# Where column-form weight blocks stand in their buffer slots: one place for all, or seven places in turn

## The chip, the cores and the metric

The kernel runs on one core of one Trainium2 chip. The metric is device time in microseconds from one launch to its end; the kernel before was run three times and took 2912.8, 2912.95 and 2913.8 us, median 2912.95. The profile is of one execution of the same program.

## The reference

The program computes two transformer-like layers on 256 tokens of width 2048, in float32. What matters here is that nearly all of the arithmetic is a token matrix times a weight matrix:

```python
h = rms_norm(x, norm_g);  proj = h @ w_in                # 2048 x 16512, split into 15 parts
ya = chunked_band_attention(aq, ak, av, a_rel_bias) * silu(az)
yb = rwkv7_time_mix(br, bk, bv, ...) * silu(bz)          # heads of 64, a scan over the tokens
yc = memory_cross_attention(cq, mk, mv) * silu(cz)       # mk, mv = rms_norm(mem) @ w_mem_kv
merged = sigmoid(ga)*(ya @ w_up_a) + sigmoid(gb)*(yb @ w_up_b) + sigmoid(gc)*(yc @ w_up_c)
x = x + merged @ w_o
# second layer: h @ w_in_2, block attention, gated linear attention, short convolution,
# three up-projections, w_out_2, then
x = x + (silu(h2 @ w_ffn_gate_2) * (h2 @ w_ffn_up_2)) @ w_ffn_down_2
return rms_norm_2(x, final_norm_w_2)
```

## The kernel before, in words

All weights are streamed once through four buffer slots. `plan_stream` (from line 57) writes the list of 128 blocks, each the product of all 256 tokens with up to 512 columns of one weight matrix; a block is cut into units, 976 in all, and unit n uses slot n modulo 4. For each unit SyncE loads float32 weights into `w_raw` (line 463), ScalarE rounds them into `w_hi` (`hi`, line 653), VectorE subtracts to get the remainder `w_lo` (`lo`, line 1058), and TensorE multiplies. Each product is three matmuls in the fp32r format: high weights by high activations, high by low, and low by high. ScalarE is told to prepare unit n + 3 while TensorE works on unit n, so the weights are ready ahead.

Blocks come in two forms. In 98 blocks of the kind `rows` the activations are the stationary operand and 512 weight columns move through the array (lines 1668 to 1670). In the other 30 blocks, the column form (kinds `wide`, `pair`, `trio` and `narrow`), a 128 x 128 tile of weights is loaded as the stationary operand and the 256 tokens move (lines 1677 to 1679). The column form gives 1,696 triples, 5,088 matmuls and as many weight loads.

A slot of `w_hi` or `w_lo` is 1,088 float32 elements (4,352 bytes) per partition, 64 more than a unit fills. `in_slot` (line 235) says where in the slot a unit's weights begin: `SHIFT` puts the `rows` kind at element 0 and the four column kinds at element 16, which is 64 bytes. ScalarE's output, both VectorE's operand and output, and TensorE's reads go through `in_slot`. The tensors begin at multiples of 512 (`w_hi`) and 256 bytes (`w_lo`), each weight tile is 512 bytes wide, so every column-form tile begins at a multiple of 64 bytes. `w_raw` is always filled and read from its slot's beginning.

The order of TensorE's work is written out by hand: between the steps of the recurrent part and of the attentions, `fill` issues units of the stream, or quarters of units (`planned_quarters`, line 1683). Waits on semaphores stand at the head of units and before the small matmuls of those parts. Nothing in the order depends on `in_slot`.

Of the kernel before, what the change touches and what calls it, by code (L numbers as in the profile page):

```python
# [48 lines left out]

SHIFT = {'rows': 0, 'wide': 16, 'pair': 16, 'trio': 16, 'narrow': 16}

DMAS = {"wide": 1, "rows": 1, "pair": 2, "trio": 2, "narrow": 1}

# [111 lines left out]
def build(nc, dram, out):  # L167
    blocks, phases, units, first = plan_stream()
# [5 lines left out]
    def last_unit(m):  # L174
        return first[m + 1] - 1 if m + 1 < len(first) else n_units - 1

    with ExitStack() as ctx:
        sem_of = {}

# [51 lines left out]
        def unit_size(n):  # L231
            k, tiles = KINDS[blocks[units[n][0]].kind]
            return k * tiles * P

        def in_slot(w, n):
            at = SHIFT[blocks[units[n][0]].kind]
            return w[:, n % RING, at:at + unit_size(n)]

        def tiles4_of(v, j):
# [11 lines left out]
        v1, v2, at = {}, {}, 0  # L251
        for name, rows in ROWS1:
            v1[name], at = at, at + rows
        n_rows1, at = at, 0
# [384 lines left out]
        def _(act):  # L639
# [7 lines left out]
            def hi(n):  # L647
                slot = n % RING
                if n >= RING:
                    act.wait_ge(sem("unit_used"), n - RING + 1)  # L650
                act.wait_ge(sem(f"landed{slot}"), landed[n])
                size = unit_size(n)
                act.activation(in_slot(w_hi, n), w_raw[:, slot, 0:size], ACT.Copy).then_inc(sem("hi_done"), 1)  # L653
# [385 lines left out]
        def _(dve):  # L1039
# [14 lines left out]
            def lo(n):  # L1054
                slot = n % RING
                dve.wait_ge(sem("hi_done"), n + 1)
                size = unit_size(n)
                dve.tensor_tensor(in_slot(w_lo, n), w_raw[:, slot, 0:size], in_slot(w_hi, n).bitcast(F32), ALU.subtract)\  # L1058
                    .then_inc(sem("lo_done"), 1)
# [575 lines left out]
        def _(pe):  # L1635
# [6 lines left out]
            def unit(n, part=None):  # L1642
# [18 lines left out]
                for j in sorted({j for j, _ in steps}):  # L1661
                    k = u * k_tiles + j
                    if b.kind == "rows":
                        wh, wl = (in_slot(w, n)[:, j * 512:(j + 1) * 512] for w in (w_hi, w_lo))
                        for a in [a for i, a in steps if i == j]:
                            o = gp[:, s, a * 512:(a + 1) * 512]
                            xh, xl = (x[k][:, a * P:(a + 1) * P] for x in (x_hi, x_lo))
                            pe.matmul(o, xh, wh, start=(k == 0), stop=False)  # L1668
                            pe.matmul(o, xl, wh, start=False, stop=False)  # L1669
                            ins = pe.matmul(o, xh, wl, start=False, stop=(k == last_k))  # L1670
                        continue
                    for c in [c for i, c in steps if i == j]:
                        o = gp[:, s, c * T:(c + 1) * T]
                        at = (j * tiles + c) * P
                        wh, wl = (in_slot(w, n)[:, at:at + P] for w in (w_hi, w_lo))

                        pe.matmul(o, wh, x_hi[k], start=(k == 0 and c % 2 == 0), stop=False, skip_group_check=True)  # L1677
                        pe.matmul(o, wh, x_lo[k], start=False, stop=False, skip_group_check=True)  # L1678
                        ins = pe.matmul(o, wl, x_hi[k], start=False, stop=(k == last_k), skip_group_check=True)  # L1679
# [422 lines left out]
```

## Time and profile before

| | before |
|---|---|
| runs | 2912.8, 2912.95, 2913.8 us; median 2912.95 |
| the profiled execution, first to last instruction | 2913.4 us |
| TensorE busy | 2882.6 us, 99% |
| VectorE, ScalarE busy | 1619.3 us (56%), 1344.1 us (46%) |
| mean granted TensorE clock | 0.999 |
| DMA | 518.30 MB, mean 178 GB/s |

The span of the profiled execution lies inside the range of the three runs, and no other time of it is recorded, so a change worked out against the span is taken off the median as it stands. TensorE's matmuls are pipelined and overlap in the profile: the duration of one (0.28 us for 256 columns) holds its whole way through the array, while the distance between the starts of two neighbours is what one costs. The two have to be kept apart below.

### The profile page before, as it was taken

What the parts mean: (1) busy time and instruction counts of PE and PEld (TensorE: products, weight loads), DVE (VectorE), ACT (ScalarE), POOL (GpSimd) and SP (SyncE); (2) the same over time, 40 slices, a digit from 0 to 9 for tenths busy, and PEclk for the clock granted to TensorE, in tenths of its full rate; (3) what the DMA queues carried; (4) which work ended last, traced back from release to release, by engine and by line L of the source; (5) the groups of instructions that cost most, each with busy time, mean ns of one, the idle gap of its engine ahead of it and who ended that gap; (6) DMA issues with size and microseconds to landing.
All of it is one profiled execution on the core that took longest, in us unless ns stands there. A gap on an engine that the chain in (4) does not pass through costs nothing.

```text
span 2913.4 us, 42709 instructions
## 1 busy us (share of the span) xinstructions
PE 2882.6 (99%) x18228; PEld 2491.1 (86%) x18228; DVE 1619.3 (56%) x1860; ACT 1344.1 (46%) x1533; POOL 73.7 (3%) x173
## 2 busy tenths in 40 slices
PE   7999999999999999999999999999999999999998
PEld 7979888888988888889998899888888888888886
DVE  5565665656656556564555466554654544544444
ACT  5452543544554454454455454444444444444443
POOL 5000000001000000000000000000000000000000
PEclk9999999999999999999999999999999999999999
DMA  7443444566665655566556566666566666666564
GB/s 211 125 143 112 134 128 118 166 195 184 227 194 184 189 163 185 191 188 182 174 161 202 166 174 174 196 194 195 192 184 195 188 193 188 188 189 206 192 194 152
DMA packets 356178, 518.30 MB, mean 178 GB/s; under 512 B 18288, under 2 KB 137220, under 8 KB 355220
## 3 DMA queue, kind: packets, MB, share of 16 engines
q1 hardware_dynamic: 355220, 512.37, 58.7%
q0 software_dynamic: 768, 3.20, 0.4%
q8 instruction: 143, 2.34, 0.3%
q14 instruction: 47, 0.39, 0.0%
HBM read 513.39 MB, written 2.11 MB: 177 GB/s over the span
## 4 chain that ended last, share of the span: by engine, by line
PE 98%; DVE 1%; ACT 0%; DMA 0%; issue 0%; SPq 0%; DVEq 0%; ACTq 0%
PE gp L1668 23%; PE gp L1670 23%; PE gp L1669 23%; PE gp L1677 7%; PE gp L1679 7%; PE gp L1678 7%; PE ps L1845 4%; PE ps L1727 1%; PE ps L1802 1%; PE ps L1833 1%; DMA gain<-in_norm_g 0%; PE ps L1787 0%; PE ps L1823 0%; PE ps L2045 0%; PE ps L2062 0%; PE ps L2053 0%
## 5 line engine op out<-in xcount | busy, mean ns | idle before, releaser
L1058 DVE TENSOR_TENSOR w_lo<-w_raw,w_hi 128x1024 fp32r<-128x1024 f32 (+2 forms) x976 | 1166.2, 1202 | 949.6 <-ACT w_hi L653 944.7
L653 ACT ACTIVATE w_hi<-w_raw 128x1024 fp32r<-128x1024 f32 (+2 forms) x976 | 1011.0, 1041 | 1106.4 <-PE gp L1670 877.7
L1668 PE MATMUL gp<-w_hi,h_hi 128*128 128x512 f32 x2112 | 833.5, 395 | 1.5 <-DVE w_lo L1058 1.5
L1670 PE MATMUL gp<-w_lo,h_hi 128*128 128x512 f32 x2112 | 822.7, 390 | 0.0
L1669 PE MATMUL gp<-w_hi,h_lo 128*128 128x512 f32 x2112 | 822.2, 389 | 0.0
L1677 PE MATMUL gp<-h_hi,w_hi 128*128 128x256 f32 x1696 | 488.4, 288 | 1.8 <-DVE h_lo L1123 1.8
L1678 PE MATMUL gp<-h_lo,w_hi 128*128 128x256 f32 x1696 | 474.5, 280 | 0.0
L1679 PE MATMUL gp<-h_hi,w_lo 128*128 128x256 f32 x1696 | 474.3, 280 | 0.0
L1668 PEld LDWEIGHTS gp<-w_hi,h_hi 128*128 128x128 f32 x2112 | 396.6, 188 | 83.8 <-DVE w_lo L1058 1.9
L1670 PEld LDWEIGHTS gp<-w_lo,h_hi 128*128 128x128 f32 x2112 | 396.5, 188 | 83.3
L1669 PEld LDWEIGHTS gp<-w_hi,h_lo 128*128 128x128 f32 x2112 | 396.8, 188 | 80.5 <-issue 0.5
L1677 PEld LDWEIGHTS gp<-h_hi,w_hi 128*128 128x128 f32 x1696 | 321.0, 189 | 8.9 <-issue 4.5
L1678 PEld LDWEIGHTS gp<-h_lo,w_hi 128*128 128x128 f32 x1696 | 321.8, 190 | 1.1 <-issue 0.5
L1679 PEld LDWEIGHTS gp<-h_hi,w_lo 128*128 128x128 f32 x1696 | 319.9, 189 | 0.0
L1668 PE MATMUL gp<-w_hi,y_hi 128*128 128x512 f32 x448 | 175.3, 391 | 0.0
L1670 PE MATMUL gp<-w_lo,y_hi 128*128 128x512 f32 x448 | 174.4, 389 | 0.0
L1669 PE MATMUL gp<-w_hi,y_lo 128*128 128x512 f32 x384 | 149.4, 389 | 0.0
L1668 PE MATMUL gp<-w_hi,f_hi 128*128 128x512 f32 x352 | 137.0, 389 | 0.0
L1670 PE MATMUL gp<-w_lo,f_hi 128*128 128x512 f32 x352 | 136.9, 389 | 0.0
L1669 PE MATMUL gp<-w_hi,f_lo 128*128 128x512 f32 x352 | 136.9, 389 | 0.0
L1845 PEld LDWEIGHTS ps<-arena 64*64 64x64 f32 x3072 | 102.8, 134 | 19.0 <-issue 10.5
L1845 PE MATMUL ps<-arena 64*64 64x32 f32 (+2 forms) x3072 | 114.7, 225 | 0.0
(290 smaller groups left out, 1805.3 us busy)
## 6 DMA issues: line engine op xcount, KB each, us to landing
w_raw<-in_w_in SPq DMA_DIRECT2D x384, 512.0 KB, 4.0
w_raw<-in_w_ffn_gate SPq DMA_DIRECT2D x88, 512.0 KB, 4.4
w_raw<-in_w_ffn_up SPq DMA_DIRECT2D x88, 512.0 KB, 4.4
w_raw<-in_w_ffn_down SPq DMA_DIRECT2D x88, 512.0 KB, 4.1
w_raw<-in_w_in SPq DMA_DIRECT2D x136, 256.0 KB, 3.2
w_raw<-in_w_in SPq DMA_DIRECT2D x128, 192.0 KB, 3.1
w_raw<-in_w_mem_kv SPq DMA_DIRECT2D x32, 512.0 KB, 4.3
w_raw<-in_w_o SPq DMA_DIRECT2D x32, 512.0 KB, 4.3
```

Source lines behind the costliest of these rows:

```text
L653: act.activation(in_slot(w_hi, n), w_raw[:, slot, 0:size], ACT.Copy).then_inc(sem("hi_done"), 1)
L1058: dve.tensor_tensor(in_slot(w_lo, n), w_raw[:, slot, 0:size], in_slot(w_hi, n).bitcast(F32), ALU.subtract)\
L1668: pe.matmul(o, xh, wh, start=(k == 0), stop=False)
L1669: pe.matmul(o, xl, wh, start=False, stop=False)
L1670: ins = pe.matmul(o, xh, wl, start=False, stop=(k == last_k))
L1677: pe.matmul(o, wh, x_hi[k], start=(k == 0 and c % 2 == 0), stop=False, skip_group_check=True)
L1678: pe.matmul(o, wh, x_lo[k], start=False, stop=False, skip_group_check=True)
L1679: ins = pe.matmul(o, wl, x_hi[k], start=False, stop=(k == last_k), skip_group_check=True)
L1727: ins = pe.transpose(cross[e % 2][:, c * T + a * P:c * T + (a + 1) * P], src[:, a, c * P:(c + 1) * P], ident[:])
L1802: ins = pe.matmul(ps[:, 2 + g % 2, tt * T + keys.start:tt * T + keys.stop], q[:, h * dt + d, tt * P:(tt + 1) * P], k[:, h * dt + d, 0:keys ...
L1833: ins = pe.matmul(psB[:, d * T + t0:(d + 1) * T], v[:, kt, at:at + P], pt[:, kt * T:(kt + 1) * T - t0], start=(kt == 0), stop=(kt == 1), s ...
L1845: ins = pe.matmul(out[hh], left[hh], right[hh], start=(i == 0), stop=(i == len(terms) - 1))
```

## The change

The table by kind is replaced by a list of places that the column-form blocks take in turn, in the order of the stream. The `rows` kind stays at element 0.

```diff
-SHIFT = {'rows': 0, 'wide': 16, 'pair': 16, 'trio': 16, 'narrow': 16}
+COLUMN_PLACES = (16, 15, 17, 14, 18, 13, 19)
...
+    place, columns = [], 0
+    for b in blocks:
+        place.append(0 if b.kind == "rows" else COLUMN_PLACES[columns % len(COLUMN_PLACES)])
+        columns += b.kind != "rows"
...
         def in_slot(w, n):
-            at = SHIFT[blocks[units[n][0]].kind]
+            at = place[units[n][0]]
             return w[:, n % RING, at:at + unit_size(n)]
```

In bytes the places are 64, 60, 68, 56, 72, 52 and 76. Of the 5,088 column-form matmuls 624 keep element 16; 864 go to element 15 and 720 each to 17, 14, 18, 13 and 19. Within a block the place is one and the same. The instructions of every engine, their order, sizes and waits stay as they are; only start addresses in `w_hi` and `w_lo` differ. The four `q_cols` blocks of the second layer, which follow each other without anything between them, are at 19, 16, 15 and 17.

## Rows read from the trace of the kernel before

**Rows 1.** The page: busy us, share of the span, instructions.
```profile
PE 2882.6 (99%) x18228; PEld 2491.1 (86%) x18228; DVE 1619.3 (56%) x1860; ACT 1344.1 (46%) x1533; POOL 73.7 (3%) x173
```
**Rows 2.** Waits of TensorE, whole span: total us, times, longest.
```profile
PE ps L1727 <- DVE arena L1136: 14.4, 2, 13.8
PE gp L1677 <- DVE h_lo L1123: 1.8, 2, 1.1
PE gp L1668 <- DVE w_lo L1058: 1.5, 1, 1.5
```
**Rows 3.** Groups by line: busy us, mean ns | idle before.
```profile
L1677 PE MATMUL gp<-h_hi,w_hi 128*128 128x256 f32 x1696 | 488.4, 288 | 1.8 <-DVE h_lo L1123 1.8
L1678 PE MATMUL gp<-h_lo,w_hi 128*128 128x256 f32 x1696 | 474.5, 280 | 0.0
L1679 PE MATMUL gp<-h_hi,w_lo 128*128 128x256 f32 x1696 | 474.3, 280 | 0.0
```
**Rows 4.** Timeline, start us and us, block of stream at 34 us.
```profile
34.37 0.28 PE L1677 MATMUL gp<-h_hi,w_hi 128*128 128x256 f32 x1
34.48 0.28 PE L1678 MATMUL gp<-h_lo,w_hi 128*128 128x256 f32 x1
...
50.69 0.28 PE L1677 MATMUL gp<-h_hi,w_hi 128*128 128x256 f32 x1
```
**Rows 5.** Timeline, the four `q_cols` blocks, entry from row form and last matmul.
```profile
1288.38 0.39 PE L1670 MATMUL gp<-w_lo,h_hi 128*128 128x512 f32 x1
1288.60 0.28 PE L1677 MATMUL gp<-h_hi,w_hi 128*128 128x256 f32 x1
...
1378.94 0.28 PE L1679 MATMUL gp<-h_hi,w_lo 128*128 128x256 f32 x1
```
**Rows 6.** Line 1678 alone, by stretches: from:to, length, PE busy (count), weight loads.
```profile
31.00:54.00 23.00, 17.92 (x65) 12.07 (x65) 1.00 0.83 229
54.00:101.00 47.00, 33.72 (x120) 22.80 (x120) 1.00 0.59 173
240.00:311.00 71.00, 35.95 (x128) 24.05 (x128) 1.00 0.42 123
1288.00:1379.00 91.00, 71.83 (x256) 49.15 (x256) 1.00 0.65 189
1664.00:1820.00 156.00, 106.92 (x384) 72.79 (x384) 1.00 0.60 166
```
**Rows 7.** Groups in 1288 to 1379 us.
```profile
L1678 PEld LDWEIGHTS gp<-h_lo,w_hi 128*128 128x128 f32 x256 | 49.1, 192 | 0.0
L1677 PEld LDWEIGHTS gp<-h_hi,w_hi 128*128 128x128 f32 x256 | 48.1, 188 | 0.0
L1679 PEld LDWEIGHTS gp<-h_hi,w_lo 128*128 128x128 f32 x256 | 48.1, 188 | 0.0
L1058 DVE TENSOR_TENSOR w_lo<-w_raw,w_hi 128x1024 fp32r<-128x1024 f32 x33 | 40.4, 1225 | 50.5 <-ACT w_hi L653 50.5
L653 ACT ACTIVATE w_hi<-w_raw 128x1024 fp32r<-128x1024 f32 x32 | 33.9, 1058 | 44.8 <-PE gp L1679 44.8
```
**Rows 8.** Timeline, entry from row form at 337 us.
```profile
337.04 0.39 PE L1670 MATMUL gp<-w_lo,h_hi 128*128 128x512 f32 x1
337.27 0.28 PE L1677 MATMUL gp<-h_hi,w_hi 128*128 128x256 f32 x1
```
**Rows 9.** Timeline, row form at 2690 us.
```profile
2690.37 0.39 PE L1670 MATMUL gp<-w_lo,f_hi 128*128 128x512 f32 x1
...
2691.73 0.39 PE L1670 MATMUL gp<-w_lo,f_hi 128*128 128x512 f32 x1
```
**Rows 10.** Groups whose operand starts off a 16-byte boundary, each above one aligned.
```profile
L674 ACT ACTIVATE xr<-gp 128x768 f32<-128x768 f32 x8 | 6.5, 810 | 13.8 <-PE gp L1679 13.8
L706 ACT ACTIVATE arena<-gp 128x768 f32<-128x768 f32 x8 | 6.5, 812 | 6.1 <-PE gp L1679 6.1
L1854 PE MATMUL ps<-xr,gain 128*128 128x256 f32 x16 | 4.7, 378 | 0.0
L2068 PE MATMUL ps<-arena,ones 128*128 128x256 f32 x16 | 4.1, 378 | 0.0
L1297 DVE TENSOR_TENSOR arena<-arena 128x260 f32<-128x260 f32 x8 | 3.4, 429 | 0.3
L1101 DVE TENSOR_TENSOR arena<-arena 128x256 f32<-128x256 f32 x8 | 3.4, 424 | 4.6 <-ACT arena L706 4.6
```
**Rows 11.** Busy of all engines in the densest column stretch, as rows 6 with DVE, ACT, POOL.
```profile
54.00:101.00 47.00, 47.00 (x429) 46.60 (x429) 35.02 (x58) 35.21 (x46) 0.00 (x0) 1.00 0.59 173
```

## The prediction, before the changed kernel was run

> **What bounds the kernel now.** I read the page's busy line first: TensorE is busy 99% of the span, VectorE 56%, ScalarE 46% [rows 1]. The waits of TensorE say the same from the other side: beyond the 14.4 us at the start there are 1.8 and 1.5 us of waiting, so almost nothing is late [rows 2]. The end is therefore set by the pace at which TensorE starts matmuls. The groups by line show three column-form lines of 1,696 matmuls each, 280 to 288 ns long [rows 3], but those durations overlap; the cost is the distance between starts, and for that I went to the timeline.
>
> There the column form turns out to have two paces. From 34.37 to 50.69 us stand 144 matmuls: 16.32 us / 144 = 113.3 ns each [rows 4]. From 1288.60 to 1378.94 us stand the 768 matmuls of the four `q_cols` blocks, 767 distances in 90.34 us: 117.8 ns each [rows 5]. The difference is 4.45 ns. Both stretches are at the full clock (1.00 in rows 6, which is 2.4 GHz), so it isn't the clock. The modelled duration of line 1678 tells the paces apart too: 17.92 / 65 = 276 ns in the quick stretch, 71.83 / 256 = 281 ns in the slow one [rows 6]. From 54 to 101 us it is 33.72 / 120 = 281, from 240 to 311 us 35.95 / 128 = 281, and from 1664 to 1820 us 106.92 / 384 = 278, a mixture [rows 6]. The slow pace also shows in the weight loads: in the slow `q_cols` stretch the load of line 1678 takes 192 ns and those of 1677 and 1679 take 188 [rows 7]. One load in three is held up by some 4 ns.
>
> A pace, once taken, stays: nothing changes it over 767 distances and four blocks. It is taken anew where TensorE restarts behind small matmuls or comes over from the row form, and both outcomes occur: from the row form at 1288.60 it becomes the slow one [rows 5], at 337.27 the quick one [rows 8]. Over the whole trace I counted 4,965 distances between neighbouring column-form matmuls: 1,934 of 113 to 115 ns, 2,840 of 116 to 119 ns and 191 others (restarts); their first and last kinds are those of rows 4 and 5. So the slow pace costs today 2,840 x 4.45 ns = 12.6 us, and the quick one would turn into a loss of 1,934 x 4.45 = 8.6 us if it were lost. The row form has one pace: from 2690.37 to 2691.73 us six matmuls, 227 ns each [rows 9]. It is not touched.
>
> **The change, part by part.** No instruction is added, removed or moved, on any engine or queue, and no wait. `w_raw` and its DMAs keep their addresses. What changes is where 4,464 of the 5,088 column-form weight tiles start (5,088 less the 624 that stay at element 16): by 4 to 12 bytes off a multiple of 64, and for all of them off a multiple of 16.
>
> ScalarE's write of `w_hi` and VectorE's read and write. In the `q_cols` stretch they take 1,058 and 1,225 ns per unit and stand idle 44.8 and 50.5 us of 91 [rows 7]; a unit of 24 matmuls takes TensorE 24 x 117.8 = 2.83 us. Unaligned ones are in the trace: ScalarE's evacuation at line 674 writes rows that begin one element past a boundary and takes 810 ns against 812 ns for the same shape at line 706; VectorE's 128 x 260 at line 1297, whose rows are 65 elements apart, takes 429 ns, and 128 x 256 at line 1101 424 ns, which is the difference of four elements [rows 10]. I take 0. Even 10% more (0.11 and 0.12 us per unit) is hidden under the rest of the 2.83 us. In the densest column stretch VectorE and ScalarE have 12 of 47 us free [rows 11], and its 16 units of 1.22 us there would ask for 2 us more. If that cover were gone, TensorE's wait for `w_lo` is what would grow; it is 1.5 us in all now [rows 2].
>
> TensorE's moving operand. The tokens keep their address. An unaligned moving operand is in the trace, `lora_x` at line 1854, 8 bytes past a 16-byte boundary: 378 ns, as line 2068 with an aligned one [rows 10]. This says that such a start need cost nothing, but of the other operand.
>
> TensorE's weight loads, the one open price. Every stationary operand of before starts on a 16-byte boundary, so no row shows the changed one. From below: the load is not what TensorE waits for, since loads of 188 ns are started every 113 ns and the next is fetched under the matmul; the price of being unaligned is then 0, and if the place breaks up the slow pace it is a gain of at most 12.6 us. From above: the only row in which something about a load costs time is the held-up one, and what hangs on it is 4.45 ns a matmul; one such step more for every moved tile is 4,464 x 4.45 = 19.9 us. I take 0, the value of the nearest row in kind (line 1854, the same engine reading the same memory unaligned), and keep -12.6 and +19.9 as ends.
>
> A rule of the Trainium skill speaks against the change. The rows say that the unaligned operands of the trace cost nothing [rows 10]. The page "SBUF — State Buffer", under "Specifications (TRN2)", says that the memory is read in lines of 16 bytes and that each crossing into a new line is paid for. A tile of 128 floats that begins on a line touches 32 lines, one that begins beside it touches 33, so by that rule each moved load would get longer by about a thirty-second. The trace doesn't agree for the moving operand and is silent on the stationary one.
>
> The paces themselves. The step from one block to the next now shifts the weights by 1 to 6 elements against the tokens, so the one thing that kept the pace over a block's end, that nothing changes, is gone there. I expect the pace to be taken anew at such steps and otherwise as now. Outside `q_cols` the present record is 1,934 quick to 2,840 - 767 = 2,073 slow, 48% quick. Redrawing these blocks with the same odds changes nothing on average. The `q_cols` blocks, one bad draw for four blocks now, become four draws: 767 x 0.48 x 4.45 ns = 1.6 us gained. By chance the sum over some 28 full blocks of about 170 counted distances varies by the root of 28 x half of 170 x 4.45 ns = 2.0 us.
>
> Sum: 0 (ScalarE, VectorE) + 0 (loads) - 1.6 (paces) = -1.6 us, 2913.4 to 2911.8 us of span; the span lies 0.45 us above the median of the runs, so the forecast is 2912.95 - 1.6 = **2911.3 us**, own range 2908 to 2915.
>
> **The rivals.** (A) *An unaligned weight load collides and the slow pace wins*; this ends slower. Its place is the weight load under a running matmul in 25 of 30 blocks. For it: one load in three already is held up in the slow pace [rows 7], and the quick pace needs a fit between two streams that the aligned start may give. Against it: line 1854, and 188 ns loads leave no sign of being near a limit. It decides once more than some 5.8 us are lost, which is 1,300 of the 1,934 quick distances. If only the quick pace is lost: +8.6 us, 2921.6 us. With one more step for every moved tile: +19.9 us, 2932.9 us. In the middle, 2927 us. By the page's line rule it would be this rival that comes true; it has the chance of this rival, since the rule gives no other time.
>
> (B) *The moved start frees TensorE from the slow pace*, at block steps or throughout; this ends clearly faster. For it: the quick pace is the one that the streams can have, the slow one has a period of three matmuls that a small shift could break, and two of the longest slow stretches (54 to 101 and 1288 to 1379 us) run over block ends that are now steps. Against it: inside a block nothing steps, and the slow pace was taken within a few matmuls of the entry at 1288.60 [rows 5]. At most 12.6 us, 2900.3 us; it has to free 1,300 of 2,840 slow distances to leave the band of no change. Middle: 2903.8 us.
>
> (C) *The place has no part in it.* The pace is taken by when TensorE restarts, not by addresses, and the same paces return: 2913 us. For it: in every column block the place was the same 64 bytes, and both paces occurred. Against it: nothing in the trace, which has never had another place.
>
> **How the numbers follow.** Forecast 34%, C 10%, A 28%, B 28%. A measurement of this kernel tells 0.2%, or 5.8 us, from no change. The forecast with its own range and C fall within it: same 0.44; A is slower, 0.28; B is faster, 0.28. For the range I go down to all of B (2900) and up into A to 2928, a little over its middle; what is left out is the upper part of A, some 12%, and a few in a hundred of surprises below.
>
> **What would show it.** Right: distances of 113 and 118 ns and nothing else in the column form, the counts moved by a few hundred, with a change of pace now found exactly at block ends inside 1288 to 1379 us; line 1678 near 280 ns; ScalarE's and VectorE's means at 1,058 and 1,225 ns within 1%; row form at 227 ns. Rival A: loads above 188 ns in blocks off element 16, distances of 118 ns or a third value there, and the 624 at element 16 as before. Rival B: `q_cols` at 113 ns and line 1678 near 276 ns overall. Rival C: all paces, stretch by stretch, as before. I am wrong altogether if the difference lies in the row form or in waits of TensorE.

## The result, and the profile after

The changed kernel takes 2919.42 us (median of 16 runs, 2918.23 to 2920.65) against 2914.16 us for the kernel before (16 runs, 2912.80 to 2915.27): 5.3 us more. The ratio is 1.0019 with a 95% interval of 1.0012 to 1.0026. It is slower, by just less than the 0.2% that the prediction called no change, and not 1.6 us faster. In its runs the time is 1.7 us above the span of the core (2918.68 us against 2917.0 for the profiled one).

The page of the changed kernel, busy us and share of the span per engine, to be read against [rows 1]:

```profile
span 2917.0 us, 42709 instructions
...
PE 2884.4 (99%) x18228; PEld 2492.8 (85%) x18228; DVE 1619.6 (56%) x1860; ACT 1344.6 (46%) x1533; POOL 71.9 (2%) x173
```

TensorE still fills the span. Its waits, against [rows 2] (total us, times, longest):

```profile
PE ps L1732 <- DVE arena L1141: 15.8, 2, 14.3
PE gp L1682 <- DVE h_lo L1128: 2.1, 3, 1.2
PE gp L1673 <- DVE w_lo L1063: 1.5, 1, 1.5
```

Lines are numbered five higher than before. The wait for `w_lo` is the same 1.5 us, so the two engines that write the weights are not late. Their groups, with those of the column form (busy us, mean ns | idle before; ScalarE's and VectorE's first):

```profile
L1063 DVE TENSOR_TENSOR w_lo<-w_raw,w_hi 128x1024 fp32r<-128x1024 f32 (+2 forms) x976 | 1166.4, 1202 | 952.9 <-ACT w_hi L658 948.4
L658 ACT ACTIVATE w_hi<-w_raw 128x1024 fp32r<-128x1024 f32 (+2 forms) x976 | 1011.4, 1041 | 1109.1 <-PE gp L1675 879.3
...
L1682 PE MATMUL gp<-h_hi,w_hi 128*128 128x256 f32 x1696 | 488.7, 288 | 2.1 <-DVE h_lo L1128 2.1
L1683 PE MATMUL gp<-h_lo,w_hi 128*128 128x256 f32 x1696 | 474.6, 280 | 0.0
L1684 PE MATMUL gp<-h_hi,w_lo 128*128 128x256 f32 x1696 | 474.5, 280 | 0.0
```

ScalarE and VectorE write and read the moved weights in the same 1,041 and 1,202 ns as before (their lines in the page of before have the same means). The matmuls' durations over the whole run, 288 and 280 ns, are also those of [rows 3]: a mean over 1,696 of them does not show the loss. The distances between starts do, and the four `q_cols` blocks, one pace of 117.8 ns before [rows 5], show how. The timeline of the changed kernel, start us and duration, at the first matmul of the first, third and fourth of these blocks and at the last of all:

```profile
1289.33 0.28 PE L1682 MATMUL gp<-h_hi,w_hi 128*128 128x256 f32 x1
...
1332.87 0.29 PE L1682 MATMUL gp<-h_hi,w_hi 128*128 128x256 f32 x1
...
1355.82 0.28 PE L1682 MATMUL gp<-h_hi,w_hi 128*128 128x256 f32 x1
...
1378.42 0.28 PE L1684 MATMUL gp<-h_hi,w_lo 128*128 128x256 f32 x1
```

At elements 19 and 16, 384 distances take 43.54 us, 113.4 ns each. At element 15, 192 take 22.95 us, 119.5 ns. At element 17, 191 take 22.60 us, 118.3 ns. The pace changes exactly at the ends of blocks, and 119.5 and 118.3 are paces that the kernel before doesn't have. Taken block by block the durations follow: 276 ns at elements 19 and 16 (from 1290 to 1332 us) and 282 ns at element 15 (from 1332.9 to 1355.7 us). The weight loads don't stand out, 189 ns each in the block at 15. The groups of these two stretches, mean ns behind the busy time:

```profile
L1683 PE MATMUL gp<-h_lo,w_hi 128*128 128x256 f32 x125 | 34.5, 276 | 0.0
...
L1683 PE MATMUL gp<-h_lo,w_hi 128*128 128x256 f32 x65 | 18.3, 282 | 0.0
...
L1682 PEld LDWEIGHTS gp<-h_hi,w_hi 128*128 128x128 f32 x64 | 12.1, 189 | 0.0
L1683 PEld LDWEIGHTS gp<-h_lo,w_hi 128*128 128x128 f32 x64 | 12.1, 189 | 0.0
```

Over the whole stream, distances from 105 to 135 ns, averaged per place, against those of the same blocks before:

| element | distances | same blocks before, ns | after, ns | product, us |
|---|---|---|---|---|
| 13 | 677 | 116.3 | 114.7 | -1.1 |
| 14 | 684 | 116.0 | 117.9 | +1.3 |
| 15 | 825 | 116.0 | 119.5 | +2.9 |
| 16 | 589 | 116.9 | 115.5 | -0.9 |
| 17 | 692 | 116.4 | 118.4 | +1.4 |
| 18 | 683 | 114.9 | 118.3 | +2.3 |
| 19 | 694 | 116.0 | 114.8 | -0.8 |

The sum is +5.1 us, against 5.3 us between the medians. Places 14, 15, 17 and 18 lose 7.9 us and places 13, 16 and 19 give back 2.8. The row form keeps its pace: its 8,824 distances from one row-form matmul to the next add up to 0.01 us more than before.

The two profiled spans differ by only 3.6 us. About 1 us more went into the start and the waits of the changed kernel (its wait for `arena` is 15.8 us against 14.4), and 2.5 us went the other way in the first 10 us of matmuls. Two units of the first block ran at double distance in the profiled execution of before. Its timeline:

```profile
18.57 0.41 PE L1678 MATMUL gp<-h_lo,w_hi 128*128 128x256 f32 x1
18.78 0.41 PE L1679 MATMUL gp<-h_hi,w_lo 128*128 128x256 f32 x1
18.99 0.41 PE L1677 MATMUL gp<-h_hi,w_hi 128*128 128x256 f32 x1
```

and that of the changed kernel:

```profile
19.02 0.28 PE L1683 MATMUL gp<-h_lo,w_hi 128*128 128x256 f32 x1
19.14 0.28 PE L1684 MATMUL gp<-h_hi,w_lo 128*128 128x256 f32 x1
19.26 0.28 PE L1682 MATMUL gp<-h_hi,w_hi 128*128 128x256 f32 x1
```

Twenty such distances were 213 ns before and 113 to 122 after. Of the kernels below, the profiles of those with element 19 or 17 everywhere have all twenty, those with 13 or 15 have none, and those with 22 everywhere or with 16, 13 and 19 in turn have ten, so I count it as no part of the change. It may be why the runs of one kernel lie in groups some 1 us apart: the profiled run of 19 everywhere, with twenty, is the slowest of its nine, but one profile per kernel doesn't prove it.

### The profile page after: what moved, and what is told of

Read it like the earlier page. It is cut to its first block, busy times and chain, and to the rows that moved or that the text cites. A ratio compares the mean times of both kernels' runs of the same rounds, so it can differ in the third digit from the quotient of the medians.

```text
span 2917.0 us, 42709 instructions
## 1 busy us (share of the span) xinstructions
PE 2884.4 (99%) x18228; PEld 2492.8 (85%) x18228; DVE 1619.6 (56%) x1860; ACT 1344.6 (46%) x1533; POOL 71.9 (2%) x173
## 4 chain that ended last, share of the span: by engine, by line
PE 98%; DVE 1%; ACT 0%; DMA 0%; issue 0%; SPq 0%; DVEq 0%; ACTq 0%
PE gp L1673 23%; PE gp L1675 23%; PE gp L1674 23%; PE gp L1682 7%; PE gp L1684 7%; PE gp L1683 7%; PE ps L1850 4%; PE ps L1732 1%; PE ps L1807 1%; PE ps L1838 1%; DMA gain<-in_norm_g 0%; DVE w_lo L1063 0%; PE ps L1792 0%; PE ps L1828 0%; PE ps L2050 0%; PE ps L2067 0%
## 5 line engine op out<-in xcount | busy, mean ns | idle before, releaser
L1063 DVE TENSOR_TENSOR w_lo<-w_raw,w_hi 128x1024 fp32r<-128x1024 f32 (+2 forms) x976 | 1166.4, 1202 | 952.9 <-ACT w_hi L658 948.4
L658 ACT ACTIVATE w_hi<-w_raw 128x1024 fp32r<-128x1024 f32 (+2 forms) x976 | 1011.4, 1041 | 1109.1 <-PE gp L1675 879.3
L1850 PE MATMUL ps<-arena 64*64 64x32 f32 (+2 forms) x3072 | 114.7, 225 | 0.0
```

The costliest lines, as they stand in the source:

```text
L1850: ins = pe.matmul(out[hh], left[hh], right[hh], start=(i == 0), stop=(i == len(terms) - 1))
```

## The experiments

The theory to test was that each place has paces of its own (P). The rivals were that it is changing places that costs (S), and that any start off a 16-byte line costs (L). All kernels below are the changed one with the edit shown.

**One place for all column-form blocks.**

```diff
-COLUMN_PLACES = (16, 15, 17, 14, 18, 13, 19)
+COLUMN_PLACES = (13,)      # and (19,), (15,), (17,)
```

Element 13: 

> Every column-form block at element 13. Theory P (each place has its own pace, whatever stood before it): the pace that the blocks at 13 have in the changed kernel, 114.7 ns a matmul against 116.0 in the kernel before, over 4,840 distances: 6.5 us less than before, about 2907.5 us, and no third pattern. Rival S (the steps from place to place cost, a constant place costs nothing): like the kernel before, 2914 us within 2. Rival L (a start off a 16-byte line costs): slower than before, the same for 13, 15, 17 and 19, by 3.6 to 20 us.

Element 19: 

> Every column-form block at element 19. Theory P: 114.8 ns a matmul as the blocks at 19 in the changed kernel, 6 us less than before, about 2908 us. Rival S: 2914 us within 2. Rival L: slower than before by the same as with 13, 15 and 17.

Element 15: 

> Every column-form block at element 15. Theory P: 119.5 ns a matmul everywhere, so 3.4 ns x 4,840 = 16.5 us more than before, about 2930.5 us. Rival S: 2914 us within 2. Rival L: slower, but by no more than with 13 and 19.

Element 17: 

> Every column-form block at element 17. Theory P: 118.4 ns a matmul everywhere, 11 us more than before, about 2925 us. Rival S: 2914 us within 2. Rival L: the same as 13, 15 and 19.

Measured, with the runs of the kernel before on the same chip at 2913.75 us: 13 took 2913.30 us (ratio 0.9998, 0.9989 to 1.0007), 19 took 2906.09 us (0.9974, 0.9964 to 0.9983), 15 took 2929.32 us (1.0052, 1.0036 to 1.0069), and 17, one run, 2926.64 us. The mean distances over all blocks were 116.05, 114.29, 119.45 and 118.36 ns. The `q_cols` blocks of each, first and last of 768 matmuls; element 13:

```profile
1284.41 0.28 PE L1682 MATMUL gp<-h_hi,w_hi 128*128 128x256 f32 x1
...
1376.44 0.28 PE L1684 MATMUL gp<-h_hi,w_lo 128*128 128x256 f32 x1
```

Element 19:

```profile
1286.64 0.28 PE L1682 MATMUL gp<-h_hi,w_hi 128*128 128x256 f32 x1
...
1373.58 0.28 PE L1684 MATMUL gp<-h_hi,w_lo 128*128 128x256 f32 x1
```

Element 15:

```profile
1293.44 0.28 PE L1682 MATMUL gp<-h_hi,w_hi 128*128 128x256 f32 x1
...
1385.09 0.28 PE L1684 MATMUL gp<-h_hi,w_lo 128*128 128x256 f32 x1
```

Element 17:

```profile
1292.98 0.28 PE L1682 MATMUL gp<-h_hi,w_hi 128*128 128x256 f32 x1
...
1383.74 0.28 PE L1684 MATMUL gp<-h_hi,w_lo 128*128 128x256 f32 x1
```

That is 120.0, 113.4, 119.5 and 118.3 ns. Theory P holds and both rivals fall: the four differ by 23 us with no change of place in any of them, so S is out, and 13 and 19 are off a 16-byte line like 15 and 17, yet reach 113.3 ns. The profile also corrects a detail of the theory. Element 15 and element 17 have one pace each: the blocks' means are 119.3 to 119.6 and 118.3 to 118.5 ns. Elements 13, 16 and 19 have two: 113.3 or 120.0 at 13 and 19, 113.3 or 117.8 at 16, taken within some twelve matmuls of the entry into a stretch and then kept (in the traces of the kernel before and of 13 and 19 everywhere, none of the 42 stretches of 36 and more distances changes its pace after that). That is why 13 missed its expected 2907.5 us by 6 us: the `q_cols` blocks alone, 767 distances at 120.0 and not 113.3, are 5.1 us. One more rival can be read from these traces: that the writes of ScalarE and VectorE into the shifted slots disturb TensorE. In the `q_cols` blocks of the kernel before, the changed one and these four, the mean distance while ScalarE or VectorE is busy is within 0.3 ns of the mean while it is idle, so the differences of 5 to 7 ns are not theirs.

**Are the steps harmless?**

```diff
-COLUMN_PLACES = (16, 15, 17, 14, 18, 13, 19)
+COLUMN_PLACES = (16, 13, 19)
```

> The change with its four slow places taken out: column-form blocks in turn at 16, 13 and 19. If the loss of the change is in the places 14, 15, 17 and 18 and not in changing places: 115.0 ns on average (115.5, 114.7 and 114.8 in the changed kernel), 5 us less than before, about 2909 us. If it is in changing places: as the changed kernel, 2919 us.

Measured 2907.84 us (before 2913.62; ratio 0.9981, 0.9971 to 0.9990), 114.9 ns on average. The step from place to place costs nothing that can be seen; taking out the four slow places (14 and 18 among them, which were not run alone) takes out the loss, with a gain on top.

**Is it the distance between weights and tokens, or the weights' own address?**

```diff
-COLUMN_PLACES = (16, 15, 17, 14, 18, 13, 19)
+COLUMN_PLACES = (17,)
...
-        h_hi = sb("h_hi", [P, KD, T], F32R, align=ROW // 2)
+        h_hi = sb("h_hi", [P, KD * T + 1], F32R, align=ROW // 2)[:, 1:].rearrange("p (a b) -> p a b", b=T)
```

and the same for `h_lo`. (Two small tensors were moved between them. By the tensors' sizes `h_lo` begins 64 elements later for it, 65 with the shift, so for its product the distance to the weights is kept only up to 64 elements; for the two products with `h_hi` it is kept exactly.)

> Column-form weights at element 17 and the tokens (h_hi, h_lo) one element past a 256-byte boundary, so that the weights stand 16 elements ahead of the tokens as in the kernel before, while their own address is that of the run with 17 everywhere. Theory R (the distance between weights and tokens decides): the column form shows the paces of place 16, 113.3 and 117.8 ns, nothing at 118.3 alone. Rival A (the weights' own address decides): 118.3 ns as with 17 everywhere, about 2926 us. The row form reads the shifted tokens as its weights; it stays at 226.7 ns if only the column form is sensitive.

Measured, one run: 2971.97 us beside 2914.76 for the kernel before, far above either expectation. The column form took 120.9 ns on average, 121.1 in the `q_cols` blocks: neither the 113.3 and 117.8 of theory R nor the 118.3 of rival A. Both fall as put. Of the 57.2 us of loss, 33.2 are in the row form's 8,824 distances, where the shifted tokens are the loaded operand. The timeline of this kernel, a row-form block that reads them, and one that reads `f_hi` and `f_lo`, which had not been moved:

```profile
2696.28 0.39 PE L1673 MATMUL gp<-w_hi,h_hi 128*128 128x512 f32 x1
...
2717.89 0.40 PE L1673 MATMUL gp<-w_hi,h_hi 128*128 128x512 f32 x1
...
2779.35 0.39 PE L1673 MATMUL gp<-w_hi,f_hi 128*128 128x512 f32 x1
...
2838.51 0.39 PE L1673 MATMUL gp<-w_hi,f_hi 128*128 128x512 f32 x1
```

The first is 93 distances in 21.61 us, 232.4 ns; the second 261 in 59.16 us, 226.7 ns, the pace of [rows 9]. Within one kernel and one form of matmul, the products with a shifted operand are the ones that are some 6 ns slower. Over 6,158 distances the mean with `h` is 232.4 ns. So the addresses of both operands of a matmul matter, and neither alone nor their distance alone gives the pace.

**The row form's place.**

```diff
-        place.append(0 if b.kind == "rows" else ...)
+        place.append((0, 3, 13, 16, 19, 32, 1)[(len(place) - columns) % 7] if b.kind == "rows" else ...)
```

with the column form at 19.

> Row-form blocks in turn at elements 0, 3, 13, 16, 19, 32 and 1, column form at 19. If the row form's 226.7 ns is a floor and its loads never meet the moving stream badly, every place runs at 226.7 ns and the time is that of 19 everywhere, 2906 us. If the row form has bad places too, some blocks run slower by about 4 to 6 ns a matmul, up to 3 us for a block of 96 matmuls in 100 us of stream, and the whole is later by 10 to 40 us.

Measured, one run: 2943.72 us, 37.6 us above 19 everywhere, so the second of the two. Means per place: 0: 227.3 ns; 19: 228.3; 3: 229.0; 16: 230.8; 32: 232.7; 13: 233.4; 1: 236.6. A block at element 1, the timeline of this kernel:

```profile
2868.13 0.40 PE L1673 MATMUL gp<-w_hi,f_hi 128*128 128x512 f32 x1
...
2929.89 0.40 PE L1673 MATMUL gp<-w_hi,f_hi 128*128 128x512 f32 x1
```

261 distances in 61.76 us, 236.6 ns against 226.7. Here the shifted operand is the one that moves, and it costs 10 ns. Element 0, where the kernel has its rows, is the best of the seven.

**Other places for the column form.** Three runs with seven places each, `COLUMN_PLACES = (0, 8, 12, 20, 22, 24, 32)` and the like.

> Column-form blocks in turn at elements 0, 8, 12, 20, 22, 24 and 32. It is read for the pace of each place. If the order seen so far (13, 16 and 19 can run at 113.3 ns, 14, 15, 17 and 18 never do) goes on in threes, 22 can run at 113.3 ns and 20 and 24 cannot. If what matters is nearness to 16, all seven run at one pace. If a start off a 16-byte line costs, only 22 is slower.

> Column-form blocks in turn at elements 10, 11, 21, 23, 28, 40 and 48, for the pace of each. In threes: 10, 28 and 40 can run at 113.3 ns, and 11, 21, 23 and 48 cannot. By nearness to 16: all alike. By 16-byte lines: 28, 40 and 48 quicker than the others.

> Column-form blocks in turn at elements 5, 25, 29, 35, 45, 51 and 54, for the pace of each. If the paces repeat every 32 elements (48 had those of 16, and 32 that of 0), 45, 51 and 54 have those of 13, 19 and 22: 113.3 as one pace. If they repeat every 16, 29 and 35 have them too. 5 and 25 have no counterpart that can run at 113.3 ns.

They took 2924.12, 2925.57 and 2925.54 us, one run each. The table has the mean of each place and the share of its distances that stand in a settled quick pace, counted as twelve or more distances of 113 or 114 ns in a row:

| places | share in the settled quick pace | mean, ns |
|---|---|---|
| 22 | 50% | 114.9 |
| 45, 48 | 51%, 37% | 115.8, 116.1 |
| 51 | 22% | 118.7 |
| 35, 11, 24, 8, 23 | none | 117.7, 117.8, 118.0, 118.3, 118.4 |
| 20, 29, 10, 32, 12 | none | 118.7, 118.7, 119.1, 119.2, 119.5 |
| 5, 0, 40, 54, 28, 25, 21 | none | 119.7, 119.8, 119.8, 119.8, 119.9, 119.9, 120.0 |

A mean over four or five blocks is rough: that of 12 is made of blocks near 118 ns and one at 123.2.

The order in threes holds near 16 (22 yes, 20 and 24 no) and fails farther off (10, 28 and 40 no, 48 yes). A repeat every 32 elements fits 48 with 16 and 45 with 13, but 51 only now and then behaves like 19, and 54 is at 120.0 where 22 is at 113.3. A repeat every 16 fits neither 29 nor 35. Rule L fails again: 0, 20, 28, 32 and 40 are on a 16-byte line and slow, 22 and 45 are off it and quick. I have no formula for the pace; that stays open.

**Element 22 everywhere.**

> Every column-form block at element 22. Its blocks in the sweep took 114.9 ns a matmul on average, with 113.3 as one pace and 116 to 118 as the other. If a place keeps its paces and the share of the quick one stays: 1.2 ns x 4,840 = 5.7 us less than before, about 2908 us. If the share is drawn anew, anything from 113.3 (2901 us) to 117.5 ns (2921 us).

Measured 2907.67 us (before 2913.62; ratio 0.9978, 0.9969 to 0.9987), 114.9 ns: as expected with the share kept.

**A version that beats both.**

```diff
-COLUMN_PLACES = (16, 15, 17, 14, 18, 13, 19)
+COLUMN_PLACES = (19, 22, 19, 19, 19, 19, 19, 19, 19, 19, 19, 19, 22, 19, 19, 19, 19, 19, 19, 22, 22, 19, 19, 19, 19, 19, 19, 19, 19, 19)
```

> Element 19 everywhere but in four blocks that ran slowly there (the second of the stream, 120.0 ns; the second of the C columns with silu, 115.1; the last two of the L columns, 115.9 and 116.0), which go to element 22, where they took 113.5, 114.7, 115.0 and 113.7 ns. If a block keeps its pace at its place: 190 distances times 6.5, 0.4, 0.9 and 2.3 ns, 1.9 us less than 19 everywhere, about 2904 us. If the pace is drawn anew at each entry: within 3 us of 2906.

Measured 2904.93 us (5 runs, 2903.32 to 2905.54) beside 2913.65 for the kernel before: ratio 0.9965, 0.9952 to 0.9979, 8.7 us less than before and 14.5 less than the changed kernel. The four blocks took 113.5, 114.7, 115.0 and 113.7 ns, each what it took at 22 alone. But the first block of the L columns, which stayed at 19, had 113.7 ns with 19 everywhere and now has 116.0, so an entry can also be redrawn without a change of place there. Between this version and 19 everywhere (2906.09 us on another chip) the runs don't decide.

## Why the prediction was wrong

*What bounds the kernel* was right: TensorE's distances between starts set the time, in two paces at element 16, kept from an entry on. After the change 99% busy and 1.5 us of waiting for weights are as before.

*ScalarE and VectorE, 0* was right: means of 1,041 and 1,202 ns before and after, no new wait.

*TensorE's weight loads, taken as 0, is the step that failed.* I left the pace of every place at what element 16 has, from the one row with an unaligned operand, line 1854, and that row says nothing here. It is of the moving operand, as the prediction itself says, and of another kind of matmul, plain float32 in place of fp32r. The timeline of before has two matmuls of line 1854 in 0.59 us and four of line 2068 in 1.03 us, one lasting 0.38 us:

```profile
178.63 0.59 PE L1854 MATMUL ps<-xr,gain 128*128 128x256 f32 x2
...
1691.38 1.03 PE L2068 MATMUL ps<-arena,ones 128*128 128x256 f32 x4
```

That is about 215 ns from start to start, unaligned or not, nearly twice the stream's 113, so the row is right about itself and was carried over to matmuls that behave otherwise. Even for a moving operand it doesn't hold in the stream: the row form at element 1 pays 10 ns. What the runs show in place of the 0: the four places 14, 15, 17 and 18, 2,884 of the 4,844 distances, run at 117.9 to 119.5 ns whatever the entry, +7.9 us. The term has neither of the values that the prediction weighed, 0 or one step for every moved tile: it differs from place to place.

*The upper end of that term* bounded it. One step of 4.45 ns for every moved tile would have been +19.9 us; 15 everywhere costs 15.6 us and 17 everywhere 12.9 us.

*The redraw of the paces, -1.6 us*, was right for the places that have a quick pace. Two of the four `q_cols` blocks went from 117.8 to 113.4 ns, and the other two stand at 15 and 17, which have none; 13, 16 and 19 together gave back 2.8 us. The expectation that a pace changes at block ends came true too, but the sign "113 and 118 and nothing else" did not: 119.5, 118.3 and mixed patterns are new.

*The band* came out by luck. The measured time lies within the 5.8 us that the prediction counts as no change, to which it gave 44% through its forecast and rival C, but neither made it so: 7.9 us lost and 2.8 given back happen to leave 5.1, and with 15 everywhere the same mechanism costs 15.6 us.

*Rival A*, an unaligned load collides and the slow pace wins, came nearest, with 5.3 us where its middle was 14, since not all unaligned places are slow. Its mechanism isn't shown: it asked for loads above 188 ns off element 16, and they average 187.8 to 188.9 ns there, no longer than the 188.6 to 189.7 of the kernel before. *Rival B* is true of single places: at 19 the kernel gains 7.7 us. *Rival C* is refuted by the four single-place runs. The line rule of the Trainium skill ("SBUF — State Buffer", "Specifications (TRN2)"), as the prediction reads it, would make all places but 16 of this change alike and slower. The measured 113.3 ns at 13, 19 and 22, and 119.8 at the aligned 0, say that it doesn't decide here, and the measurement goes before the page.

*The base.* I took 2913.4 us of span as the whole of the profiled execution; in all later profiles the run is 1.7 us longer than the span, and the median of 16 runs of before is 2914.16. This moved the forecast by 1.2 us, no part of the error in sign.

That each place has its own price is shown, by seven places in one kernel and five of them alone. How two operand streams come to disturb each other at some addresses is not. That it happens inside TensorE's own reading is argued: the waits for weights didn't grow, the distances are the same whether ScalarE and VectorE are busy or idle, and in the row form the slower pace followed the shifted tensor.

## What to carry to other kernels

Where TensorE is the bound, measure the distance between starts stretch by stretch, since a mean duration over all matmuls of a line can stay at 280 ns while blocks go from 276 to 282, and compare it with the quickest distance that the same shape reaches anywhere in the trace; a few ns on thousands of matmuls are worth a search over buffer offsets of single elements. One run with seven offsets in turn prices seven of them, if each is read by its own blocks and has one pace (15 and 17: 119.5 and 118.4 ns in turn as well as alone). An offset that has two paces must be judged over the whole kernel (13: 114.7 ns in turn, 116.05 alone), since the pace is taken at the entry into a stretch, and an offset found good for one operand's address holds for that address only.

## What the runs showed of the hardware that had not been expected

- The distance between fp32r matmuls of 256 columns depends on the start address of the loaded operand to the single element: settled paces of 113.3 to 120.0 ns, and 123.2 in one block at element 12, at otherwise equal work and granted clock 1.00. Alignment to 16, 32 or 64 bytes doesn't predict it.
- Some offsets have one pace, others two or more between which the entry decides (22 has 113.3, one near 116.7, and 120.0 ns); a pace holds over 767 distances.
- The row form (512 columns moving) depends on both operands' addresses as well: 226.7 ns at the kernel's own, 232.4 with the loaded operand one element on, 236.6 with the moving one.
- At the start of the profile of before, 20 distances took 213 ns where the changed kernel had 113 to 122 ns, though the granted clock of that stretch is given as 1.00. The stretch in the kernel before (from:to, length, busy us and count of PE, PEld, DVE, ACT and POOL, granted clock, DMA share, GB/s):

```profile
18.00:23.00 5.00, 4.15 (x18) 3.89 (x19) 4.52 (x7) 1.03 (x2) 3.79 (x11) 1.00 0.81 236
```

and in the changed one, where 22 matmuls start in place of 18:

```profile
18.00:23.00 5.00, 2.72 (x22) 2.56 (x23) 4.98 (x7) 1.18 (x2) 3.85 (x10) 1.00 0.66 189
```
